# Delta network's lengths by a stationary block of ones in four column groups, and the small projections with stationary weights in four column groups

## The reference

```python
proj = h @ w_in          # h: 512 x 1024
(q_att, c_kv, q_idx, k_idx, w_idx, qkv, a, b, z, gates) = jnp.split(proj, SPLITS, axis=-1)
...
rel = jax.nn.relu(jnp.einsum('bqhd,bsd->bqhs', qi, k_idx))
iscore = jnp.einsum('bqhs,bqh->bqs', rel, wi)       # wi: from w_idx, 8 columns
...
qkv = jax.nn.silu(causal_conv(qkv, conv_w))         # 3 x 1024 channels, width 4
q = l2_normalize(qkv[..., :1024].reshape(B, S, 8, 128)) * (128 ** -0.5)
k = l2_normalize(qkv[..., 1024:2048].reshape(B, S, 8, 128))
beta = jax.nn.sigmoid(b)                            # b: 8 columns
g = -jnp.exp(a_log) * jax.nn.softplus(a + dt_bias)  # a: 8 columns
```

## Time and profile before

| | |
|---|---|
| median of 3 runs | 2203.62 us (2201.04 to 2203.65) |
| profiled execution | 2201.36 us |
| its span, first to last instruction | 2199.7 us |
| TensorE busy | 2142.6 us, 97%, 9737 matmul records |
| VectorE, ScalarE, GpSimd busy | 1065.5, 463.5 and 140.1 us |
| data moved | 385.40 MB, 175 GB/s in the mean |
| mean granted TensorE clock | 0.985 |

### The profile page before, as it was taken

The page is one execution under the profiler, slowest core; times in us unless marked ns, Lnnn a source line. Parts: engine busy times, 40 slices in busy tenths (PEclk is TensorE's granted clock), DMA queues, the critical chain, the costliest instruction groups (busy, mean ns, idle before and its releaser), DMA issues.

```text
span 2199.7 us, 25312 instructions
## 1 busy us (share of the span) xinstructions
PE 2142.6 (97%) x9737; PEld 1446.7 (66%) x9737; DVE 1065.5 (48%) x1960; ACT 463.5 (21%) x990; POOL 140.1 (6%) x274
## 2 busy tenths in 40 slices
PE   9999999999999999999999999999998999999997
PEld 4447884768888787545756579888855544544552
DVE  4675675578888623295335855433555111111115
ACT  2134211122222101124536423211001000000002
POOL 0000000000100000000101031000000100000001
PEclk9999999999999999999999999999998999999999
DMA  4247122335553312112121111322352899999997
GB/s 166 77 152 241 39 79 83 145 125 181 187 180 129 112 73 77 62 53 87 68 77 58 58 39 73 115 77 96 134 210 115 354 428 428 428 421 427 427 427 301
DMA packets 46122, 385.40 MB, mean 175 GB/s; under 512 B 7145, under 2 KB 7273, under 8 KB 20777
## 3 DMA queue, kind: packets, MB, share of 16 engines
q1 hardware_dynamic: 31536, 317.39, 36.7%
q0 software_dynamic: 14176, 49.06, 6.4%
q10 hardware_dynamic: 289, 17.30, 2.3%
HBM read 369.54 MB, written 35.68 MB: 184 GB/s over the span
## 4 chain that ended last, share of the span: by engine, by line
PE 92%; DMA 4%; DVE 2%; DVEq 1%; issue 1%; ACT 1%; SPq 0%; ACTq 0%
PE banks L667 29%; PE banks L1671 13%; PE banks L2965 9%; PE banks L780 8%; PE banks L534 6%; PE banks L3093 5%; PE banks L2978 4%; PE banks L1788 4%; PE banks L1910 3%; DMA arena<-in_experts 2%; DMA ring<-in_experts 2%; PE banks L837 1%; PE banks L853 1%; PE banks L789 1%; PE banks L1747 1%
## 5 line engine op out<-in xcount | busy, mean ns | idle before, releaser
L667 PE MATMUL banks<-ring 128*128 128x256 f32 x1568 | 363.5, 380 | 5.1 <-ACT ring L743 3.0
L667 PEld LDWEIGHTS banks<-ring 128*128 128x128 f32 x1568 | 298.3, 191 | 47.2 <-ACT ring L743 4.6
L667 PE MATMUL banks<-arena,ring 128*128 128x256 f32 x1400 | 326.5, 380 | 0.4 <-DVE banks L749 0.4
L667 PEld LDWEIGHTS banks<-arena,ring 128*128 128x128 f32 x1400 | 266.4, 191 | 37.6 <-issue 1.3
L1671 PE MATMUL banks<-arena,ring 128*128 128x512 f32 x656 | 287.7, 597 | 0.0
L1671 PEld LDWEIGHTS banks<-arena,ring 128*128 128x128 f32 x656 | 124.1, 192 | 148.8 <-issue 147.6
L780 PE MATMUL banks<-arena,ring 128*128 128x512 f32 x448 | 193.9, 593 | 1.5 <-DVE arena L1101 1.5
L780 PEld LDWEIGHTS banks<-arena,ring 128*128 128x128 f32 x448 | 85.2, 191 | 108.6 <-issue 106.3
L3093 PEld LDWEIGHTS banks<-arena 128*128 128x128 f32 x1024 | 119.7, 196 | 30.1 <-issue 28.8
L1977 ACT ACTIVATE arena<-banks 128x512 f32<-128x512 f32 (+4 forms) x151 | 80.0, 534 | 244.3 <-PE banks L667 85.9
L3093 PE MATMUL banks<-arena 128*128 128x128 f32 x1024 | 125.6, 283 | 5.6 <-issue 4.5
(11 more groups left out here) (402 smaller groups left out, 2412.8 us busy)
## 6 DMA issues: line engine op xcount, KB each, us to landing
arena<-in_experts SPq DMA_DIRECT2D x52, 2048.0 KB, 23.5
ring<-in_stream SPq DMA_DIRECT2D x94, 1024.0 KB, 4.8
ring<-in_experts SPq DMA_DIRECT2D x44, 2048.0 KB, 21.8
arena<-in_w_adaT POOLq DMA_DIRECT2D x48, 512.0 KB, 4.6
ring<-in_down SPq DMA_DIRECT2D x16, 704.0 KB, 5.4
expert_results<-arena POOLq DMA_DIRECT2D x60, 128.0 KB, 7.5
arena<-modulation_rows POOLq DMA_DIRECT2D x5, 512.0 KB, 5.1
arena<-in_xT SPq DMA_DIRECT2D x2, 1024.0 KB, 6.1
```

The lines of the kernel that those rows point to most:

```text
L667: m = pe.matmul(out, weights[:, k * P:(k + 1) * P], moving[:, k, :], start=first and k == 0, stop=k == 3, skip_group_check=True)
```

## The change

**Small projections.** The small weights become the stationary operand, 32 columns of them (24 used), and 512 tokens of `h` move. The eight matmuls, one for each 128 input channels, write to four groups of 32 partitions of one bank (`sp`), k modulo 4, each group adding two of them. ScalarE copies the bank to `PB_`. Behind gemm `ck` 0, four matmuls (`sm`) take 128 columns of that copy as the weights and move a "stacked identity", 128 x 32 with a one where row modulo 32 is the column, which adds the four groups and turns the result to tokens on the partitions. GpSimd makes that matrix with three additions at the start of the program. ScalarE takes the tables apart with three operations instead of twelve, now behind `ck` 0.

**`kb`.** Its sixteen one-column matmuls are no longer in a row, but two of them stand ahead of each matmul of gemm `qi` 1.

**Lengths.** Squares go to six buffers instead of four. After gemms 4, 8, 12 and 16 four matmuls with 32 columns of ones as weights move 512 tokens' squares each, one head for each group of 32 partitions (`l2`). ScalarE copies the bank, and one gemm later four transposes turn it (`lt`). ScalarE takes one column of each 32 for the lengths. `DC_ORDER`, the decays, the key and query products and all of VectorE's program stay as they are.

The diff, cut to its core:

```diff
@@ -360,6 +360,7 @@
         self.route_w = self.sb("route_weights", [P, DT, NG + NE])
+        self.stack = self.sb("stacked_identity", [P, BLK])
         self.route = self.view(RT_, ROUTE)
@@ -1434,6 +1435,11 @@
+def lengths_at(i):
+    return i // 4 - 1 if i % 4 == 0 and 4 <= i <= 16 else None
 def decays_at(i):
@@ -1491,11 +1497,11 @@
     p.align(8)
-    small = p.weights(column_blocks(w, D, ("small",)))
-    for t in range(TT):
-        p.job("sm", t, "act", shared=(small, 8))
+    p.job("sp", 0, "act", column_blocks(w, D, ("small",)))
     for t in range(2):
         p.job("ck", t, "act", column_blocks(w, D, span(C_CK + t * P)))
+        if t == 0:
+            p.job("sm", 0, "act")
     p.job("ssck", 0, "act")
@@ -1523,8 +1529,10 @@
         p.job("dc", t, "dve", column_blocks(w, D, span(C_DN + t * P)))
-        if 2 <= i < 18:
-            p.job("l2", DC_ORDER[i - 2], "act")
+        if lengths_at(i) is not None:
+            p.job("l2", lengths_at(i), "act")
+        if lengths_at(i - 1) is not None:
+            p.job("lt", lengths_at(i - 1), "act")
         if i == 3:
@@ -1625,7 +1633,11 @@
 def squares_view(c, i):
-    return c.view((W_ + 1024, W_ + 1536, QE_, QE_ + 512)[i % 4], S)
+    return c.view((W_ + 1024, W_ + 1536, QE_, QE_ + 512, ST_, ST_ + 512)[i % 6], S)
+def lengths_view(c, m):
+    return c.view(XC_ if m < 3 else ST_, S)
@@ -1676,24 +1688,39 @@
     pe.wait_ge(*c.bank_free("kb", 0))
+    pe.wait_ge(*c.bank_free("qi", 1))
     pe.wait_ge(c.sem("mod"), 1)
-    for j, name in enumerate(("ki", "qi")):
-        for k in range(DT):
+    at = c.plan.first["qi", 1]
+    for k in range(DT):
+        for j, name in enumerate(("ki", "qi")):
             m = pe.matmul(c.bank("kb", 0)[:, j:j + 1], c.weight(c.plan.first[name, 0] + k), c.mod[:, k:k + 1],
-                          start=k == 0, stop=k == DT - 1)
+                          start=k == 0 and j == 0, stop=k == DT - 1, skip_group_check=True)
+        if k == DT - 1:
+            m.then_inc(done, 1)
+        if k == 0 or (at + k) % CHUNK == 0:
+            pe.wait_ge(*c.landed(at + k))
+        pe.wait_ge(c.sem("h"), k + 1)
+        m = pe.matmul(c.bank("qi", 1), c.weight(at + k), h[:, k, :], start=k == 0, stop=k == DT - 1)
     m.then_inc(done, 1)
-    for t in range(1, 4):
-        gemm("qi", t, lambda k: h[:, k, :], DT, ready="h" if t == 1 else None)
+    for t in range(2, 4):
+        gemm("qi", t, lambda k: h[:, k, :], DT)
+    pe.wait_ge(*c.bank_free("sp", 0))
+    bank, at = c.bank("sp", 0), c.plan.first["sp", 0]
+    pe.wait_ge(*c.landed(at))
+    for k in range(DT):
+        r = k % 4 * BLK
+        m = pe.matmul(bank[r:r + BLK, :], c.weight(at + k)[:, 0:BLK], h[:, k, :], start=k < 4, stop=k >= 4)
+    m.then_inc(done, 1)
+    gemm("ck", 0, lambda k: h[:, k, :], DT)
+    part = c.view(PB_, S)
+    pe.wait_ge(*c.bank_free("sm", 0))
+    pe.wait_ge(*c.put_away("sp", 0))
+    pe.wait_ge(c.sem("stacked"), 1)
     for t in range(TT):
-        pe.wait_ge(*c.bank_free("sm", t))
-        bank = c.bank("sm", t)
-        pe.wait_ge(*c.landed(c.plan.first["sm", t]))
-        for k in range(DT):
-            m = pe.matmul(bank[:, 0:24], h[:, k, t * P:(t + 1) * P],
-                          c.weight(c.plan.first["sm", t] + k)[:, 0:24], start=k == 0, stop=k == DT - 1)
-        m.then_inc(done, 1)
-    for t in range(2):
-        gemm("ck", t, lambda k: h[:, k, :], DT)
+        m = pe.matmul(c.bank("sm", 0)[:, t * BLK:(t + 1) * BLK], part[:, t * P:(t + 1) * P], c.stack[:, :],
+                      start=True, stop=True)
+    m.then_inc(done, 1)
+    gemm("ck", 1, lambda k: h[:, k, :], DT)
     sums(c, pe, ("ssck", 0), 2, lambda k: sq[:, k, :], "squares2", squares)
@@ -1798,15 +1825,22 @@
         gemm("dc", t, lambda k: h[:, k, :], DT)
-        if 2 <= i < 18:
-            u = DC_ORDER[i - 2]
+        u = lengths_at(i)
+        if u is not None:
             pe.wait_ge(*c.bank_free("l2", u))
-            bank = c.bank("l2", u)
-            squares[0] += 1
+            squares[0] += 4
             pe.wait_ge(c.sem("squares2"), squares[0])
+            for r in range(4):
+                m = pe.matmul(c.bank("l2", u)[r * BLK:(r + 1) * BLK], c.ones[:, 0:BLK], squares_view(c, 4 * u + r),
+                              start=True, stop=True)
+            m.then_inc(done, 1)
+        u = lengths_at(i - 1)
+        if u is not None:
+            pe.wait_ge(*c.bank_free("lt", u))
+            pe.wait_ge(*c.put_away("l2", u))
             for k in range(TT):
-                m = pe.matmul(bank[:, k:k + 1], squares_view(c, i - 2)[:, k * P:(k + 1) * P], c.ones[:, 0:1],
-                              start=True, stop=True)
+                m = pe.transpose(c.bank("lt", u)[:, k * P:(k + 1) * P], lengths_view(c, u)[:, k * P:(k + 1) * P],
+                                 c.ident[:, :])
             m.then_inc(done, 1)
@@ -1986,19 +2020,19 @@
         put("qi", t, qi[:, t, :])
-    for t in range(TT):
-        a.wait_ge(*c.finished("sm", t))
-        bank = c.bank("sm", t)
-        if t == 0:
-            a.wait_ge(c.sem("mod_rows"), 16)
-        a.activation(tokens(sm, WI_S)[:, t, :], bank[:, 0:8], ACT.Copy, scale=INDEX_SCALE)
-        a.activation(tokens(sm, ARAW_S)[:, t, :], bank[:, 8:16], ACT.Copy)
-        a.activation(tokens(sm, BETA_S)[:, t, :], bank[:, 16:24], ACT.Sigmoid).then_inc(c.emptied("act", "sm", t), 1)
+    put("sp", 0, c.view(PB_, S))
     for t in range(2):
...
         a.activation(ck[:, t, :], bank, ACT.Copy).then_inc(c.emptied("act", "ck", t), 1)
+        if t == 0:
+            a.wait_ge(c.sem("mod_rows"), 16)
+            a.wait_ge(*c.finished("sm", 0))
+            bank = c.bank("sm", 0)[:, 0:TT * BLK].rearrange("p (t j) -> p t j", t=TT)
+            a.activation(tokens(sm, WI_S), bank[:, :, 0:8], ACT.Copy, scale=INDEX_SCALE)
+            a.activation(tokens(sm, ARAW_S), bank[:, :, 8:16], ACT.Copy)
+            a.activation(tokens(sm, BETA_S), bank[:, :, 16:24], ACT.Sigmoid).then_inc(c.emptied("act", "sm", 0), 1)
     put("ssck", 0, rstd, ACT.Sqrt, bias=c.cons[:, 0:1], scale=1.0 / CKV)
@@ -2085,14 +2119,20 @@
             a.drain()
-            if i >= 4:
-                a.wait_ge(*c.finished("l2", DC_ORDER[i - 4]))
+            if i >= 6:
+                a.wait_ge(*c.finished("l2", (i - 6) // 4))
             if i == 2:
...
             a.activation(squares_view(c, i), qkv[:, t, :], ACT.Square).then_inc(sem("squares2"), 1)
-        if 2 <= i < 18:
-            u = DC_ORDER[i - 2]
-            put("l2", u, tokens(sm, SQ_S if u < 8 else SK_S)[:, :, u % 8], cols=TT)
+        u = lengths_at(i)
+        if u is not None:
+            put("l2", u, lengths_view(c, u))
+        u = lengths_at(i - 1)
+        if u is not None:
+            a.wait_ge(*c.finished("lt", u))
+            bank = c.bank("lt", u).rearrange("p (t r j) -> p t r j", t=TT, r=4)
+            a.activation(tokens(sm, SK_S if u < 2 else SQ_S)[:, :, 4 * (u % 2):4 * (u % 2) + 4], bank[:, :, :, 0],
+                         ACT.Copy).then_inc(c.emptied("act", "lt", u), 1)
         if i == 3:
@@ -2199,7 +2239,7 @@
     moving_sums(c, v, h, c.mixed())
-    v.wait_ge(*c.put_away("sm", TT - 1))
+    v.wait_ge(*c.put_away("sm", 0))
     v.wait_ge(c.sem("decay_params"), 32)
@@ -2385,7 +2425,7 @@
         if i == 10:
-            v.wait_ge(*c.put_away("l2", DC_ORDER[7]))
+            v.wait_ge(*c.put_away("lt", 1))
             v.tensor_scalar(rk, sm[:, SK_S:SK_S + 32], EPS, None, ALU.add)
@@ -2403,7 +2443,7 @@
         if i == 20:
-            v.wait_ge(*c.put_away("l2", DC_ORDER[15]))
+            v.wait_ge(*c.put_away("lt", 3))
             v.tensor_scalar(power_q, power_q, P * EPS, P * EPS * EPS, ALU.mult, ALU.add)
@@ -3404,6 +3444,13 @@
                     pattern=[[-1, P]], channel_multiplier=1).then_inc(c.sem("constants"), 1)
+    g.drain()
+    g.tensor_tensor(c.stack[:, :], c.ident[:, 0:BLK], c.ident[:, BLK:2 * BLK], ALU.add)
+    for at in (2 * BLK, 3 * BLK):
+        g.drain()
+        m = g.tensor_tensor(c.stack[:, :], c.stack[:, :], c.ident[:, at:at + BLK], ALU.add)
+    m.then_inc(c.sem("stacked"), 1)
+    g.drain()
...
```

## The result

| | before | after |
|---|---|---|
| median | 2202.33 us (2198.38 to 2203.65, 4 runs) | 2179.84 us (2178.87 to 2183.69, 4 runs) |
| profiled execution | 2201.36 us | 2180.25 us |
| its span | 2199.7 us | 2178.6 us |
| mean granted TensorE clock | 0.985 | 0.991 |

The ratio is 0.991 with a 95% interval from 0.9893 to 0.9927: 22.5 us faster, where 15.1 were forecast. A later comparison on one chip, 6 runs of the changed kernel beside 23 of the one before, gave 17.7 us (2199.64 to 2181.98, ratio 0.992, 0.9903 to 0.9937); one of the 23, at 3216.51 us with a granted clock of 0.651, counts in no ratio. So the first question is what of the 22.5 belongs to the change.

What follows compares the result with a forecast made beforehand. TensorE, 92% of the chain of waits, was taken to bound the kernel. Gains of 7.65 us (small projections) and 7.5 (lengths), 15.1 together, off the 2203.62 us median gave 2188.5 us, range 2185 to 2195.

Steps and rivals of the forecast that it cites:

- by the price per record it is the same 3.5 us: Small projections: the sixteen `kb` matmuls, interleaved with `qi` 1, cost as much as in a row, so nothing gained.
- The wait for VectorE's taps before gemm 14: Middle of the `dc` stretch: TensorE, now earlier, waits 0.8 us for the bank of gemm 13.
- The whole `dc` stretch: Lengths: 8.3 us gross gain less a 0.8 us wait, net 7.5 us.
- the edges: Going in and out of narrow matmuls: 0.1 us at each edge, 0.2 a visit.
- The merge doesn't wait for GpSimd: End of the `dc` stretch: GpSimd's first two spread inverses are ready at 1279.8, the second needed at 1281.1.
- Loads that show: Four-group sets: a load hides under one other record only; six sets cost 1.3 us, 2189.8; chance 0.10.
- two at a time: Four-group sets: only neighbouring records overlap; gains 5.9 and 4.8 us, together 10.7, 2192.9; chance 0.13.
- one after another: Four-group sets: no overlap; 2.5 us gained in the projections, -2.0 in the lengths, 2203.1; chance 0.03.
- The middle takes over: `dc` stretch: ScalarE, VectorE and GpSimd come less early than forecast; with 3 us, 2191.5; chance 0.08.
- Narrow records read as idleness: 32-column sets: clock falls at all five places; 2220 one after another, 2205.6 four at a time; chances 0.03 and 0.02.
- the Trainium skill's 3.07x: Four-group sets: 3.07x speedup, not 4x; 0.26 us more a set, six sets 1.6 us, 2190.1.

Runs made afterwards that it cites:

- the last experiment: The changed kernel with the 154 us gap filled, the third lengths block put away by VectorE, and an early dummy square root: 2178.36 us, ratio 0.9906.

## Why the prediction was right and wrong

The direction and the two mechanisms of the forecast gain were right. The time came out 8.7 us under the 2188.5 forecast and below the range, and three things make that up: a base that was too high, a saving that the prediction had put at nothing, and a low first measurement.

**The base, 3.9 us.** I set the sum against a median of three runs, 2203.62 us. Three later batches of 16 to 23 runs gave 2199.64, 2199.78 and 2199.84 for the same kernel. From 2199.7 the same sum gives 2184.6. The range went down by the spread that three runs showed, 2.6 us; the 22 runs of one later batch spread over 11.6 us, and the twelve beside them over 13.3.

**The step that failed, 3.2 us: "by the price per record it is the same 3.5 us".** I took `kb` interleaved to gain nothing, because the earlier trace rows show the one-column row at full clock. They do, for that execution, and for it the step is right (24.17 us from `kb` to `sm` in either form). In the other five traces with `kb` in a row the clock falls there, for 6.8 us in four and 3.4 in one. Interleaving then takes 3.35 us out of `kb` to `sm`, shown in both kernels. Against the traces with both falls the projections gain 51.72 - 40.85 = 10.87 us and not 7.65; against the mean of the five old traces they gain 9.9, and the step is worth 2.2 us. The one trace also served as an argument against a rival ("3.49 us of one-column records left the clock at 1.00"), and that argument was worth less than it looked: short records in a row do lower the clock here. What saved the forecast from that rival is that four groups of 512 columns don't: the clock is 1.00 at `sp` and no trace has a fall in the `dc` stretch.

**The draw, 2.1 us.** The first four runs of the changed kernel had a median of 2179.84, the next six 2181.98; whether chance or another chip made the difference isn't known. These three make 9.3 us (taking 3.2 for the step). Against them stand 0.7 that the lengths gained less and 0.2 behind `qa`, so some 0.3 are left over. That they sum so well is in part luck, since the first and the last are differences of medians in a spread of 6 to 13 us.

Term by term, measured against forecast:

- `sp` 1.86 us for 1.92, `sm` 0.81 for 0.89, the two `ck` gemms 13.92 for 13.74. From 902.15 to the end of `ck` 16.59 for 16.55, so 24.20 - 16.59 = 7.61 us gained for 7.65. The entry edge, 0.09 in the gemm ahead of `sp`, comes off that: 48.37 - 40.85 = 7.52 in the first pair. This term stands, the 3.4 us of the clock in it included.
- A block of lengths with both edges 1.19 us for 1.06, its transposes 0.44 for 0.45.
- The wait for VectorE's taps before gemm 14, 1.0 us for 0.8.
- The whole `dc` stretch 6.78 us for 7.5, in each pair of traces. The new visits cost 4 x (1.19 + 0.44) = 6.5 us for 6.0 and the wait 0.2 more, which are the missing 0.7. That leaves 6.78 + 1.0 + 6.5 = 14.3 us for the sixteen old visits, 0.89 each, as taken from the earlier trace rows. The term that was mis-sized is the edges: 0.2 a visit, read off the experts' rows, left out what the record behind the narrow ones costs; they are 0.33 (1.19 - 0.86).
- The merge doesn't wait for GpSimd: its `expand` of the first two inverses starts at 1259.24 and takes 6.99 us, done at 1266.23, and TensorE is there at 1266.89. So the second inverse is done 0.7 us before TensorE begins the merge, where I had counted 0.4.
- `qa` to `dc` is 0.18 us longer, forecast at nothing; in the last experiment it is 135.70 again. Nothing behind the merge is longer, and the whole earlier start reaches the end (909.7 to 910.7 us from `vt` on in all four traces).

**The rivals.** Loads that show, two at a time and one after another fall with 1.86 and 1.00 us: the excess over 1.72 and 0.86 is 0.14 us for two rounds of four as for one, so no load shows in a round. One after another was also built, and cost 9.2 us. "Two at a time" rested on the order of records in the queue, and with neighbours in one group that order cost 0.02 us. The middle takes over: no. Narrow records read as idleness: no fall in 32-column sets. By the Trainium skill's 3.07x on top of my edges a block would have cost 1.32 us; it cost 1.19, between that and my 1.06.

By stages the change is worth 10.9 + 6.8 - 0.2 = 17.5 us, and 16.5 with the mean of the old traces. The 17.7 of the repeated comparison has an interval of about 14 to 21 us (0.9903 to 0.9937) and holds both. The first pair's 22.5 had 5 to 6 us in it that the change didn't make; its traces have 6.25 us ahead of `kb`, from the clock at 156 us.

## What to carry to other kernels

A sum over the partitions with a single moving column costs about a weight load for each record (0.112 us, one column or 128). Turned round, with ones as a narrow stationary block, four such sums in four column groups and their transposes cost 1.63 us here, where they cost 4 x 0.89 = 3.56. When you price a narrow set, count the record ahead of it and the record behind it. Look at several traces of the kernel before you call a stretch clean: the clock over a row of short matmuls differed between executions, and a step priced from one trace at nothing was worth 3.4 us in four of the other five. Where short matmuls can't be avoided, put them between long ones.

## What the hardware showed

- Within thirty-two one-column records in a row (3.5 us at full clock) the granted clock fell to 1.2 GHz for 6.8 us in four traces of six, for 3.4 us in one and not at all in one; with the same records in groups of four between pairs of 512-column ones it never did, in 8 traces.
- Four float32 matmuls with 32 columns of weights, 512 moving, in four column groups cost 1.19 us with both edges instead of 3.74 in one group. With neighbours in one group, 1.88 us for eight instead of 1.86.
- The edges of such a set: 0.09 us in the 128-column record ahead of it, 0.10 in the one behind it, and 0.14 in the set (1.00 us for 0.86).
- The clock fall at 156 us, behind TensorE's wait for ScalarE, lasted 0, 3.4, 6.8, 10.2, 13.7 or 17.1 us in the eleven traces with that wait unfilled, and the times of one and the same program spread over 0.6%, the longest at the lowest mean clock.
